# Two tensors take another place in SBUF: the split activations h_hi and h_lo, ahead of the squares instead of behind the small tensors

## The reference

```python
def first_block(x, c, ...):
    mod = (silu(c) @ w_mod + b_mod)                 # six vectors
    h = rms_norm(x, norm_mix) * (1.0 + scale_m) + shift_m
    z = h @ w_in
    # sliding-window attention, a gated recurrence and block attention on slices of z
    merged = g[:, :, 0] * p_a + g[:, :, 1] * p_b + g[:, :, 2] * p_c
    x = x + gate_m * (merged @ w_out)
    h = rms_norm(x, norm_ffn) * (1.0 + scale_f) + shift_f
    u = causal_dwconv(h @ w_up, ffn_conv_w, ffn_conv_b)
    return x + gate_f * ((silu(u_gate) * u_val) @ w_down)

def second_block(x, mem, ...):
    for l in range(2):
        h = rms_norm_2(x, ng[0]); x = x + 0.5 * rms_norm_2(swiglu(h, ...), ng[1])
        h = rms_norm_2(x, ng[2]); x = x + rms_norm_2(mixer_block(h, ...), ng[3])
        h = rms_norm_2(x, ng[4]); x = x + rms_norm_2(cross_attention(h, mem_n, ...), ng[5])
        h = rms_norm_2(x, ng[6]); x = x + 0.5 * rms_norm_2(swiglu(h, ...), ng[7])
    return x
```

## Time and profile before

| | |
|---|---|
| median of three runs | 2536.27 us (2535.03 to 2538.09) |
| profiled execution, own time | 2538.09 us |
| profiled execution, span | 2536.3 us |
| mean granted clock of TensorE | 0.961 |
| PE busy | 2346.4 us, 93% |
| DVE busy | 1719.5 us, 68% |
| ACT busy | 1324.3 us, 52% |
| POOL busy | 388.5 us, 15% |
| DMA | 400.41 MB, mean 158 GB/s |

### The profile page before, as it was taken

One profiled execution on the slowest core, in us unless ns is written; L12 is line 12 of the kernel. 1 busy time (PEld: TensorE's weight loads), 2 busy tenths in 40 slices (PEclk: granted clock), 3 DMA queues, 4 the chain that ended last, 5 costly groups with the idle time before them and its releaser, 6 DMA issues.

```text
span 2536.3 us, 44221 instructions
## 1 busy us (share of the span) xinstructions
PE 2346.4 (93%) x18041; PEld 2244.7 (89%) x18041; DVE 1719.5 (68%) x2425; ACT 1324.3 (52%) x2074; POOL 388.5 (15%) x354
## 2 busy tenths in 40 slices
PE   6998898999998998999898998998988989898997
PEld 5977898999998987889898998998987889898997
DVE  5666886886664896886555654664897887555663
ACT  2565445764444654664635445444654765635443
POOL 1000000110110564430000110110564530000110
PEclk9998999999999998999999999999998999999998
DMA  8534584566654452446344654655462345443652
GB/s 246 164 109 141 169 254 143 183 205 207 189 181 150 151 184 82 125 133 194 117 139 125 187 184 137 184 182 167 135 198 75 120 133 183 132 142 118 190 177 81
DMA packets 402041, 400.41 MB, mean 158 GB/s; under 512 B 18006, under 2 KB 399304, under 8 KB 401841
## 3 DMA queue, kind: packets, MB, share of 16 engines
q1 hardware_dynamic: 399457, 389.27, 49.5%
q0 software_dynamic: 2384, 8.32, 1.1%
HBM read 396.45 MB, written 1.09 MB: 157 GB/s over the span
## 4 chain that ended last, share of the span: by engine, by line
PE 68%; DVE 21%; ACT 6%; issue 4%; DMA 1%; ACTq 0%; POOL 0%; DVEq 0%; POOLq 0%
PE gemm_ps L842 57%; DVE weights_lo L1421 6%; DVE y L1857 5%; PE misc_ps L913 2%; PE gemm_ps L845 2%; PE misc_ps L970 2%; PE misc_ps L969 2%; ACT weights_hi L1099 1%; DVE mod_partial L1518 1%; ACT L1103 1%; ACT e L1218 1%; DVE y L1574 1%; DVE x_res L1576 1%; DVE neg_max L1620 1%; ACT h_hi L1170 1%
## 5 line engine op out<-in xcount | busy, mean ns | idle before, releaser
L1421 DVE TENSOR_TENSOR weights_lo<-raw_weights,weights_hi 128x1024 fp32r<-128x1024 f32 x704 | 858.2, 1229 | 467.1 <-ACT weights_hi L1099 463.2
L842 PE MATMUL gemm_ps<-h_hi,weights_hi 128*128 128x256 f32 x3664 | 1057.2, 289 | 71.5 <-DVE h_lo L1555 46.1
L1099 ACT CAST weights_hi<-raw_weights 128x1024 fp32r<-128x1024 f32 x704 | 719.7, 1033 | 649.8 <-PE gemm_ps L842 600.8
L842 PE MATMUL gemm_ps<-h_lo,weights_hi 128*128 128x256 f32 x3664 | 1038.9, 284 | 0.0
L842 PE MATMUL gemm_ps<-h_hi,weights_lo 128*128 128x256 f32 x3664 | 1037.0, 283 | 0.0
L842 PEld LDWEIGHTS gemm_ps<-h_hi,weights_hi 128*128 128x128 f32 x3664 | 704.3, 192 | 85.1 <-issue 68.8
L842 PEld LDWEIGHTS gemm_ps<-h_lo,weights_hi 128*128 128x128 f32 x3664 | 704.4, 192 | 4.0 <-issue 3.0
L842 PEld LDWEIGHTS gemm_ps<-h_hi,weights_lo 128*128 128x128 f32 x3664 | 702.4, 192 | 0.0
L1986 POOL TENSOR_TENSOR y<-y,prod 128x256 f32<-128x256 f32 x240 | 251.2, 1047 | 348.6 <-ACT prod L1359 196.2
L1974 POOL TENSOR_TENSOR hidl<-hf,hidh 128x512 fp32r<-128x512 f32 x55 | 73.5, 1336 | 1278.9 <-ACT hidh L1343 1278.9
L842 PE MATMUL gemm_ps<-hidh,weights_hi 128*128 128x256 f32 x880 | 247.8, 282 | 0.3 <-DVE weights_lo L1421 0.3
(11 more groups left out here) (282 smaller groups left out, 2826.0 us busy)
## 6 DMA issues: line engine op xcount, KB each, us to landing
raw_weights<-in_ffn_w_dram SPq DMA_DIRECT2D x256, 512.0 KB, 3.6
raw_weights<-in_w_in_dram SPq DMA_DIRECT2D x200, 512.0 KB, 3.7
raw_weights<-in_w_mod_dram SPq DMA_DIRECT2D x48, 512.0 KB, 5.0
raw_weights<-in_w_up_dram SPq DMA_DIRECT2D x44, 512.0 KB, 4.6
raw_weights<-in_xattn_kv_dram SPq DMA_DIRECT2D x32, 512.0 KB, 3.7
raw_weights<-in_w_out_dram SPq DMA_DIRECT2D x24, 512.0 KB, 4.6
raw_weights<-in_w_down_dram SPq DMA_DIRECT2D x20, 512.0 KB, 5.0
raw_weights<-in_w_branch_dram SPq DMA_DIRECT2D x16, 512.0 KB, 4.1
```

What stands on the lines that cost most here:

```text
L842: mm = pe.matmul(ps[:, c, 0:T], w[:, m, kt, c * P:(c + 1) * P], x[:, f, :], start=start, stop=stop_)
L1099: act.copy(WH[s], RAWB[:, u["raw"] % RAW, 0:u["nkt"], 0:u["cols"]]).then_inc(sems["weights_rounded"], 1)
L1421: dve.tensor_tensor(WL[s], RAWB[:, u["raw"] % RAW, 0:u["nkt"], 0:u["cols"]], WH[s], ALU.subtract).then_inc(sems["weights_rest"], 1)
```

## The change

One line is moved up by 13 lines, from behind the last small tensors to ahead of `squares`:

```diff
     X, Y = sb("x_res", [P, NF, T]), sb("y", [P, NF, T])
+    HH, HL = sb("h_hi", [P, NF, T], F32R), sb("h_lo", [P, NF, T], F32R)
     SQ = sb("squares", [P, NF, T])
 ...
     NM, DEN, RD, ES = sb("neg_max", [P, 4]), sb("den", [P, 4]), sb("rden", [P, 4]), sb("sink_exp", [P, 4])
-    HH, HL = sb("h_hi", [P, NF, T], F32R), sb("h_lo", [P, NF, T], F32R)
```

## The result

The changed kernel took 2552.23 us (median of six runs, 2547.89 to 2557.76) against 2535.99 (six runs, 2534.70 to 2538.09): a ratio of 1.0062, with a 95% interval of 1.0048 to 1.0077. It is 16 us slower; the forecast was no change, and 2552 lies outside its range of 2531 to 2542. The profiled execution took 2549.33 us, with a span of 2547.5.

What follows compares the result with a forecast made beforehand. The prediction took PE to bound the kernel (busy 93% of the span, 68% of the chain). Its three terms, each 0, summed to 0 on a span of 2536.3 us, so it forecast 2536.3 us, range 2531 to 2542.

Steps and rivals of the forecast that it cites:

- the first term: PE's 11,520 products reading h at its new place keep their pace: 0, bounds 23 us slower to 35 us faster.
- the twins: PE reads of h_hi, hidh, h_lo and hidl at other addresses, 279 or 280 ns each, taken as showing addresses harmless.
- My third term: Squares, reciprocal roots, parameter columns and other small tensors move up 16,384 bytes: 0, with a bound of 4.6 us.
- the bound of 35 us: Faster end for products reading h, from medians of 276 ns on line 845 against 279 on line 842.
- the two bounds: For products reading h: 23 us slower (line 845's 281 ns against 279) and 35 us faster (its 276 against 279).
- The place of `h` collides: PE's reads of h wait for nearby ACT or DVE accesses; 2 ns a product gives 2559 us; chance 0.03.
- The old place costs something that goes: h_hi's old start on an odd multiple of 64 bytes slowed PE's reads; up to 35 us faster, 2501; chance 0.03.
- Falls of the clock: More or fewer clock falls where PE pauses; one 10 us fall gives 2541 or 2531; 0.02 each way past the limit.
- The start within a pair of words: A row's start off an 8-byte boundary slows reads; no moved tensor changes that remainder, so 2536; no separate chance.
- The other terms: ACT and DVE writes of h at the new place, 0 within 0.4 us, and the moved small tensors, 0 within 4.6 us.

Runs made afterwards that it cites:

- a_h64: The changed kernel with h_hi, h_lo and all behind them 64 bytes higher, and 64 more bytes ahead of the shared area; 2523.44 us, ratio 0.9952.
- k_new64: The changed kernel with 64 bytes of small tensors allocated ahead of h instead of behind it; 2533.15 us, ratio 0.9990.
- l_old0: The kernel before with 64 bytes of small tensors allocated behind h instead of ahead of it; 2553.76 us, ratio 1.0071.
- e_all192: The changed kernel with h 192 bytes higher and 128 more bytes ahead of the shared area; 2513.61 us, ratio 0.9917.
- n_192_64: The changed kernel with a 128-byte gap between weights_hi and weights_lo and 64 bytes of small tensors ahead of h; 2484.43 us, ratio 0.9806.

## Why the prediction was wrong

**The step that failed is the first term, "11,520 x 0".** Its count, and the claim that the whole case hangs on this pace, held. Its price was wrong: 120.0 - 117.7 = 2.3 ns in the stretch of the earlier trace rows, 2.2 over the long piece (2.24 us over the 1,008 of its 1,272 products that read `h`). All 11,520 would make 25 us; 16 were measured. That the rest was covered where DVE or ACT set the end fits DVE's share of the chain, which fell from 21% to 15%; no run isolates it. The profiled execution shows still less, 11.2 us of span, with a mean clock of 0.966 against 0.961; how much of the gap the clock accounts for is not shown.

**Why the twins misled.** I called it evidence that `h`, `hidh` and the rows and slots behind their starts lie at many addresses and take one time. They do, but all these addresses are alike in what counts. The rows of `h` are 1024 bytes apart, the slots of the weights 4096 and their tiles 512 (four slots of four rows with two tiles each, so 32 starts and not sixteen); 115,392 and 131,776 leave the same remainder by 256, and so do the starts of both halves of the weights. The sample had one distance, 64, over and over. The change moved `h` by 25,152, which is 98 x 256 + 64, out of that class. My third term had the same flaw, and there it did no harm, as the shift of 16,384 is a multiple of 256.

**The one row that did differ was explained away.** On line 845 the roles are turned, so the streamed weights lie 192 past the activation where it lies 64 past the weights. Its median was 276 ns with `h`, and it was this row that gave the bound of 35 us. I wrote that the two bounds "contradict each other in sign" and that the durations differ "by what stands around them and not by the place". The table turned round bears the row out: in `a_h64`, line 845 with `h` (streamed minus stationary: 192) ran at 114.6 ns, and with `mh` (64) at 117.8, where line 842 with `mh` (192) was at 114. The rows of `a_h64`, first the one order of operands (line 844 there), then the other (line 847):

```profile
L844 PE MATMUL gemm_ps<-mh,weights_hi x128: 276/276/775, 1223.5 to 2203.0; 128*128 128x256 f32 x128
```

```profile
L847 PE MATMUL gemm_ps<-weights_hi,h_hi x176: 273/276/1202, 135.0 to 1863.8; 128*128 128x256 f32 x160, 128*128 128x128 f32 x16
...
L847 PE MATMUL gemm_ps<-weights_hi,mh x128: 277/279/470, 1260.4 to 2263.8; 128*128 128x256 f32 x128
```

It was the effect itself, in the trace of before.

That trace held the second pace too. I took 5.65 us for 48 products of line 845 as its pace. The piece of the same line just ahead, with the same operands (`mh`, streamed minus stationary: 192), took less, in the same view:

```profile
1272.49 5.45 PE gemm_ps L845 x48
```

That is 113.5 ns a product, with a median record of 276 ns, where the piece of the earlier trace rows has 117.7 and the 281 of the earlier trace rows. So the two bounds, 276 and 281, were the two paces of one distance. Over the whole trace of before, line 845 ran at 114.4 ns with `h` and at 115.7 with `mh`, against 117.6 and 117.8 on line 842.

**The rivals.** *The place of `h` collides* had the right sign and the right place to look, and its test (a pace above 117.8, a median on `h` off by 1 ns with `hidh` as before) is what happened; I gave it 0.03. Its mechanism was wrong: `k_new64` has the same neighbours but for 64 bytes and no cost, `l_old0` the old neighbours and the cost. What I held against it, that ACT and DVE write the weights while PE reads them without a loss, is true and beside the point, since the other side is PE's own weights and not these writes. Here the Trainium skill ("SBUF — State Buffer", section "Who interferes with whom") was taken to exclude any wait of TensorE. It gives TensorE two independent read ports, for the streamed operand and for the weights, and one rule, that only the pair shared by VectorE and GpSimd contends. On other engines' writes the trace after agrees with it: products kept 120 ns with and without them. But these runs show that the distance between PE's own two operands changes the pace by up to 6%, so they are not independent here, and for this the measurement decides. Whether they meet at a port or behind it no run shows. *The old place costs something that goes* is refuted in the form given (an odd multiple of 64): `l_old0` puts `h` on a multiple of 128 in the old region and is slower. *Falls of the clock*: the mean of the profiled execution went up, not down, and cannot have made it slower. *The start within a pair of words* was not tested: no run moved a tensor by anything but a multiple of 8 bytes.

**The other terms.** The writes of `h` stayed within 4 ns, ACT's 403 at 403 and DVE's 420 at 416, and every other engine within 2 us of busy time: these zeros held.

## What to carry to other kernels

A twin is evidence only if it differs in what the change changes: before calling an address harmless, write down the remainders, here by 256, of all operands that one engine reads together, and look whether they vary at all. Where PE works without a break, allocating a few dozen bytes between the weights and the streamed operand is an experiment worth making early; it cost no instruction and gave 1.9% here. And a median that differs from its twins by one per cent over 176 products at full clock is a finding to follow up, not noise.

## What the runs showed of the hardware that was not expected

- Back to back products of 128 x 128 by 256 columns in this format ran at mean paces between 113.3 and 120.0 ns, by the distance of the streamed operand from the weights modulo 256 (0 and 256 alike, and 0 and 512 alike, to 0.1 ns).
- The effect has a sign: exchanging which operand is streamed exchanges the paces of 64 and 192.
- At 192 two paces exist for the same addresses, 113.3 and 117.8 ns, and a stretch keeps its own until a pause; the faster one occurs at 64 too, for 3 to 8% of the products with `h`. The runs of `e_all192`, with all at 192, spread over 21 us against 5 in `n_192_64`; that the two paces cause this was not shown.
- The writes of ACT and DVE into the very weights that PE reads changed neither pace: 120 ns with and without them in the kernel after, 117.7 to 117.8 in the kernel before.
- With the halves of the weights at 192 and 64 the pace was 113.3 ns for some nine in ten of the products with `h`, and most stretches that began slower reached it within a dozen products.
